# A ring of eight weight granules instead of four, with the low parts written over the raw weights

## What is computed

```python
u = rms_norm(h, mix_norm_pre[layer]); u = even_mixer(...) or odd_mixer(...)   # u @ w_in, attention, @ w_out
h = h + rms_norm(u, mix_norm_post[layer])
u = swiglu(rms_norm(h, ffn_norm_pre[layer]), w_gate, w_up, w_down)
h = h + rms_norm(u, ffn_norm_post[layer])
...
# third layer
hn = rmsnorm(h, norm_gain); proj = hn @ w_in
ya = pool_mixer(...) * silu(pool_gate); yb = ssm_mixer(...) * silu(ssm_gate)   # gelu, @ w_glu, sigmoid inside
h = h + concat([ya, yb]) @ w_out
h = h + (p @ w_ple) * sigmoid(h @ w_ple_gate)
return rmsnorm(h, final_gain)
```

## Time and profile before

| | |
|---|---|
| median of 3 executions | 3060.84 us (3059.07 to 3060.97) |
| span of the profiled execution | 3056.1 us, 3.0 to 4.9 us below the three times |
| PE busy | 2929.4 us, 96% of the span |
| DVE, ACT busy | 1733.2 us (57%), 1417.3 us (46%) |
| DMA | 515.45 MB, 169 GB/s over the span |
| granted TensorE clock | 0.986 on average |

### The profile page before, as it was taken

One profiled execution on the slowest core, in us unless ns is written; L12 is line 12 of the kernel. 1 busy time (PEld: TensorE's weight loads), 2 busy tenths in 40 slices (PEclk: granted clock), 3 DMA queues, 4 the chain that ended last, 5 costly groups with the idle time before them and its releaser, 6 DMA issues.

```text
span 3056.1 us, 34851 instructions
## 1 busy us (share of the span) xinstructions
PE 2929.4 (96%) x13709; PEld 2409.1 (79%) x13709; DVE 1733.2 (57%) x2222; ACT 1417.3 (46%) x1809; POOL 74.0 (2%) x66
## 2 busy tenths in 40 slices
PE   8999999999999999999999999999999998888998
PEld 7878878788888888878877788888888876656776
DVE  5775655544544454554445544544445569988545
ACT  5543375544444444454446544444444454343444
POOL 0000000000000000000000000000000021210000
PEclk9999999999999999999999999999999999989999
DMA  6532235555555555555552555555555553324543
GB/s 232 176 125 93 87 138 196 179 191 185 190 193 193 193 180 192 193 178 186 187 178 97 181 198 189 182 193 192 193 192 192 181 176 112 97 91 159 179 154 124
DMA packets 255293, 515.45 MB, mean 169 GB/s; under 512 B 8240, under 2 KB 8464, under 8 KB 254144
## 3 DMA queue, kind: packets, MB, share of 16 engines
q1 hardware_dynamic: 252896, 501.61, 48.4%
q0 software_dynamic: 2272, 12.10, 1.1%
HBM read 511.58 MB, written 2.10 MB: 168 GB/s over the span
## 4 chain that ended last, share of the span: by engine, by line
PE 86%; DVE 9%; ACT 3%; issue 2%; DMA 0%; SPq 0%; DVEq 0%; ACTq 0%
PE acc L464 79%; PE side L655 2%; DVE u L1606 2%; DVE u L2207 1%; DVE pc L1606 1%; DVE wlo L1618 1%; ACT ar L1006 1%; DVE ar L1606 1%; PE side L521 1%; DVE ar L1609 1%; PE side L766 1%; ACT whi L1017 1%; PE side L550 1%; ACT xh L1006 0%; ACT L1006 0%
## 5 line engine op out<-in xcount | busy, mean ns | idle before, releaser
L1618 DVE TENSOR_TENSOR wlo<-raw,whi 128x1024 fp32r<-128x1024 f32 x948 | 1156.4, 1226 | 1124.0 <-ACT whi L1017 1123.1
L1017 ACT ACTIVATE whi<-raw 128x1024 fp32r<-128x1024 f32 x948 | 997.9, 1060 | 1232.0 <-PE acc L464 1230.8
L464 PE MATMUL acc<-whi,xh 128*128 128x512 f32 x3072 | 1220.6, 397 | 55.6 <-DVE wlo L1618 49.3
L464 PE MATMUL acc<-whi,xl 128*128 128x512 f32 x3072 | 1204.4, 392 | 0.0
L464 PE MATMUL acc<-wlo,xh 128*128 128x512 f32 x3072 | 1204.1, 392 | 0.0
L464 PEld LDWEIGHTS acc<-whi,xh 128*128 128x128 f32 x3072 | 582.2, 190 | 187.6 <-DVE wlo L1618 37.3
L464 PEld LDWEIGHTS acc<-whi,xl 128*128 128x128 f32 x3072 | 581.5, 189 | 123.5
L464 PEld LDWEIGHTS acc<-wlo,xh 128*128 128x128 f32 x3072 | 582.5, 190 | 117.1
L464 PE MATMUL acc<-whi,hTh 128*128 128x512 f32 x720 | 281.1, 390 | 2.7 <-ACT u L1006 2.7
L464 PE MATMUL acc<-wlo,hTh 128*128 128x512 f32 x720 | 280.8, 390 | 0.0
L464 PE MATMUL acc<-whi,hTl 128*128 128x512 f32 x720 | 280.8, 390 | 0.0
(11 more groups left out here) (227 smaller groups left out, 1345.2 us busy)
## 6 DMA issues: line engine op xcount, KB each, us to landing
raw<-in_ffn_w_gate SPq DMA_DIRECT2D x88, 1024.0 KB, 5.0
raw<-in_ffn_w_up SPq DMA_DIRECT2D x88, 1024.0 KB, 5.0
raw<-in_ffn_w_down SPq DMA_DIRECT2D x88, 1024.0 KB, 5.0
raw<-in_ev_w_in SPq DMA_DIRECT2D x56, 1024.0 KB, 4.9
raw<-in_od_w_in SPq DMA_DIRECT2D x48, 1024.0 KB, 5.1
raw<-in_w_in SPq DMA_DIRECT2D x32, 1024.0 KB, 5.4
raw<-in_ev_w_out SPq DMA_DIRECT2D x16, 1024.0 KB, 5.0
raw<-in_od_w_out SPq DMA_DIRECT2D x16, 1024.0 KB, 5.0
```

What stands on the lines that cost most here:

```text
L464: mm = pe.matmul(acc[2 * pair + t][:], x[:, k0 + j, tok], w[:, ring, j], start=first and j == 0 and n == 0, stop=last and j == 1 and n == 2)
L1017: act.activation(whi[:, place % RING], raw_granule(place), ACT.Copy).then_inc(S("hi_done"), 1)
L1618: dve.tensor_tensor(wlo[:, place % RING], raw_granule(place), whi[:, place % RING].bitcast(F32), ALU.subtract).then_inc(S("lo_done"), 1)
```

## The change

The low parts get no tile of their own: DVE writes them over the raw weights they were made from. The room that becomes free goes to the high parts, so that `whi` holds eight granules. `raw` still has four slots of two granules each (SLOTS), and a slot is loaded again only when PE has used both its granules (`used`, where `lo_done` was). ACT may split granule g once PE has used g-8, if its slot has landed. The place of evacuations and leads, `after`, goes from 2 to 4 in ACT's and DVE's `granules`; ev_sb keeps its own value of 3 on ACT, and the up stages have their places written out (2) and keep them. In glu, with 4 granules in a chunk, the place becomes 3.

```diff
-RING = 4
+SLOTS = 4
+RING = 2 * SLOTS
...
-        raw = sb("raw", [RING, 4, CH])
+        with nc.sbuf_tensor("wlo", [P, RING, 2, CH], F32R) as wlo:
+            pass
+        raw = sb("raw", [RING, 2, CH])
         whi = sb("whi", [RING, 2, CH], F32R)
-        wlo = sb("wlo", [RING, 2, CH], F32R)
...
-                ring = n % RING if ring is None else ring
-                if not isinstance(n, int) or n >= RING:
-                    sp.wait_ge(S("lo_done"), 2 * n - 2 * RING + 2)
-                sp.dma_start(raw[:, ring], src).then_inc(S(f"landed{ring}"), 16)
+                ring = n % SLOTS if ring is None else ring
+                if not isinstance(n, int) or n >= SLOTS:
+                    sp.wait_ge(S("used"), 2 * n - RING + 2)
+                sp.dma_start(raw[:, 2 * ring:2 * ring + 2].rearrange("p g k n -> p (g k) n"), src)\
+                    .then_inc(S(f"landed{ring}"), 16)
...
-                                sp.wait_ge(S("lo_done"), 2 * (n0 + m) - 2 * RING + 2)
-                            sp.dma_start(raw[:, (n0 + m) % RING, 2 * c:2 * c + 2], w[:, 2 * m + c])\
+                                sp.wait_ge(S("used"), 2 * (n0 + m) - RING + 2)
+                            sp.dma_start(raw[:, 2 * ((n0 + m) % SLOTS) + c], w[:, 2 * m + c])\
...
                 if not isinstance(g, int) or g >= RING:
                     act.wait_ge(S("used"), g - (RING - 1))
-                act.activation(whi[:, place % RING], raw_granule(place), ACT.Copy).then_inc(S("hi_done"), 1)
+                act.activation(whi[:, place], raw_granule(place), ACT.Copy).then_inc(S("hi_done"), 1)
...
-            def granules(name, evac, lead, aside=None, after=2):
+            def granules(name, evac, lead, aside=None, after=4):
...
-                dve.tensor_tensor(wlo[:, place % RING], raw_granule(place), whi[:, place % RING].bitcast(F32),
+                dve.tensor_tensor(wlo[:, place], raw_granule(place), whi[:, place].bitcast(F32),
                                   ALU.subtract).then_inc(S("lo_done"), 1)
...
-            def granules(name, evac, lead, aside=None, after=2):
+            def granules(name, evac, lead, aside=None, after=4):
```

More of the change, by code:

```diff
@@ L244, in _ @@
                                                       bass.ds(first * CH + i * CH, CH)]
-                            slot(n0 + m + 8 * i, src, m % RING)
+                            slot(n0 + m + 8 * i, src, m % SLOTS)
                 elif name == "ple":
@@ L263, in raw_granule @@
         def raw_granule(place):
-            return raw[:, place // 2, 2 * (place % 2):2 * (place % 2) + 2]
+            return raw[:, place]
         def landed(eng, g):
@@ L272, in landed @@
             else:
-                before = sum(1 for k in range(GRAN0["ple"] // 2, GRAN0["pg"] // 2) if k < n and k % RING == n % RING)
-                eng.wait_ge(S(f"landed{n % RING}"), 16 * (n // RING + 1 - before))
+                before = sum(1 for k in range(GRAN0["ple"] // 2, GRAN0["pg"] // 2) if k < n and k % SLOTS == n % SLOTS)
+                eng.wait_ge(S(f"landed{n % SLOTS}"), 16 * (n // SLOTS + 1 - before))
         def tab(ct):
@@ L786, in block_of @@
                                 features_use(name, h)(0, j)
-                            granule(i * 16 + (g0 + 8 * m + j), j % RING, m, xh, xl, 2 * j, j == 0, j == 7)
+                            granule(i * 16 + (g0 + 8 * m + j), j, m, xh, xl, 2 * j, j == 0, j == 7)
                 block_of(0, True)
@@ L1011, in split @@
                 if place is None:
-                    place = g % (2 * RING)
+                    place = g % RING
                     if g % 2 == 0 or GRAN0["ple"] <= g < GRAN0["pg"]:
@@ L1331, in block_of @@
                                 n = (g0 + 8 * m + j) // 2
-                                act.wait_ge(S(f"landed{n % RING}"), i * 32 + 16 * (n // RING + 1))
+                                act.wait_ge(S(f"landed{n % SLOTS}"), i * 32 + 16 * (n // SLOTS + 1))
                             split(i * 16 + (g0 + 8 * m + j), j)
@@ L1614, in split @@
             def split(g, place=None):
-                place = g % (2 * RING) if place is None else place
+                place = g % RING if place is None else place
                 dve.wait_ge(S("hi_done"), g + 1)
-                dve.tensor_tensor(wlo[:, place % RING], raw_granule(place), whi[:, place % RING].bitcast(F32),
+                dve.tensor_tensor(wlo[:, place], raw_granule(place), whi[:, place].bitcast(F32),
                                   ALU.subtract).then_inc(S("lo_done"), 1)
```

## The result

The changed kernel takes 3065.11 us (median of 20 runs, 3059.85 to 3069.15), the kernel before, run between them, 3060.06 us (20 runs, 3057.68 to 3062.42). The ratio is 1.0016, with a 95% interval of 1.0010 to 1.0022: slower by 5.05 us. The interval tells that from none, though it is less than the 6.1 us that the forecast took for about what a measurement of this kernel can tell from none. The prediction was 3065.5 us.

A forecast was written before the change was run, and what follows sets the result against it. PE, busy 96% of the span, was taken as the bound, with only about 127 us idle to touch. Terms -7.5 + 7.5 - 2.8 + 1.1 + 4.9 + 1.5 = +4.7 us gave 3065.5 us, own range 3059 to 3071.

The forecast's parts named there:

- the steady state: Up and dn stages: PE does not wait there now, so the deeper ring brings 0.
- Delta rule: Beside ev_sb: ACT's splits no longer held up, copies start when their source is ready; -7.5 us, bounds 0 and -11.2.
- rival D: Delta rule: copies start early but PE then waits for DVE in the same places; sum +12.2, 3073 us, chance 0.15.
- Leads: Stage starts od_in, s_in, od_out, ev_out, s_out: leads come later, behind granule 4's split; together +7.5 us, bounds 0 and 10.
- splits behind them: Behind the leads: two more splits are ready, so waits such as 0.79 us at od_in's granule 3 go; -2.8 us.
- s_in's chunk 0: s_in, chunk 0: the evacuation comes behind a split and PE's turn waits for it; +1.1 us, which stays.
- it lands at T0 - 0.5: Leads: the slot of granules 4 and 5 lands 0.5 us before T0, the end of the stage before.
- Rival E: Up and dn stages: slot loads now and then take 9 us or more and stall PE; 3078 us, chance 0.12.
- glu's chunk 2: glu: glu_out(1) goes behind pool_group(3) and one split, so PE waits longer; +4.9 us, bounds 3.7 and 6.2.
- The clock: glu: after its longer idle spell PE begins chunk 2 at the lower clock level; +1.5 us, 0 to 3.4.
- rival B: Leads and half of glu's loss are hidden, delta rule gives its full 11.2 us; -10.4, 3050 us, chance 0.14.
- Rival C: s_in's state space rounds: eight PE waits of 4.7 us would go; -37, 3024 us, chance 0.04.

The follow-up runs named there:

- experiment 4: The changed kernel with evacuations and leads behind granule 2 and ACT splitting granule g only when g-4 is used: 3060.14 us, ratio 0.9999 to the kernel before.
- experiment 2: The changed kernel with evacuations and leads back behind granule 2 everywhere, ring of eight kept: 3050.15 us, ratio 0.9969 to the kernel before.
- experiment 5: The kernel before, with ACT's two copies of a turned ev_sb chunk put ahead of the split of granule 6: 3056.16 us, ratio 0.9987.
- Experiment 1: The changed kernel with the evacuations of glu alone back behind granule 2: 3056.89 us, ratio 0.9987 to the kernel before.
- experiment 8: The kernel before, ring of four, with only glu's evacuation and lead moved behind granule 4, a chunk's last: 3070.78 us, ratio 1.0036.
- experiment 7: The changed kernel with evacuations and leads behind granule 3 up to the second feed-forward, behind granule 2 from s_in on: 3047.26 us, ratio 0.9961.
- experiment 3: The changed kernel with evacuations and leads behind granule 3 everywhere: 3054.2 us, ratio 0.9980 to the kernel before.
- experiment 6: The changed kernel with GpSimd's loads of x and c_odd, which ran beside ev_out's first weights, issued later: 3060.96 us, ratio 1.0003 to the kernel before.

## Why the prediction was right, point by point

**The subtraction in place, 0, and the steady state, 0: right.** 1221 ns a split, and experiment 4, which keeps both, is at 0.9999 of before.

**Delta rule, -7.5: right in its mechanism, too small, and bounded by a row read wrongly.** The stages show -10.2 us, experiment 2 -10.7 by medians, and experiment 4 that ACT's held splits were the cause. The bound of 11.2 us took the earlier trace rows for PE's idle time, where they add that of the weight loads to that of the matmuls: for the matmuls ACT's two parts were 7.7 us, in five places. The "three places" for DVE were one pause counted twice, at 207.7 us, and the weight loads' side of a pause that the matmuls' side puts down to ACT's copy, at 310.1. PE's idle time in this part fell by 8.8 us (12.9 to 4.2), more than the 7.7, and its busy time by 1.4, which no row here explains. The step that was mis-sized is "where its chain ends just behind ACT's copy, little is won", for which I had taken a third off. There is one such place, at 310.1 us, and experiment 5, where PE still waits 1.28 us there, shows that it counts while the ring is one of four. With the ring of eight it does not, and at 207.7 us DVE's wait falls from 2.11 to 0.92. That DVE's own splits come earlier, since ACT's do, and that so its chain starts earlier is argued, not shown step by step; experiments 4 and 5 show that it hangs on ACT's held splits and not on the five pairs of copies. So rival D, whose premise was that DVE would hold PE in the same places, is refuted for the new ring; it had got a chance of 0.15.

**Leads, +7.5, splits behind them, -2.8, and s_in's chunk 0, +1.1: the sum of +5.8 was near, the parts were not all.** By PE's waits, od_in has +2.0 us (forecast 1.9), s_in +2.0 (2.2) and s_out +1.7 (1.7). od_out has nothing (0.6): PE waits 0.31 us there in both kernels. ev_out has +3.1 (1.1). The waits for a split behind the leads, 0.79 us twice and 0.43 three times, are gone: -2.9. In s_in, ACT makes PE wait 1.04 us before the turn, as forecast, yet "it stays" was wrong: a wait of 1.1 us at granule 17 went in exchange. That is +5.8 in all, the forecast's sum, with ev_out's excess of 2.0 us made up by od_out and s_in. The step that failed is "it lands at T0 - 0.5": I used the median of 48 loads in another stage for a slot that meets 2.4 MB of GpSimd's, and it landed at 475.4 us, 1.2 us behind ev_z's last matmul. Rival E had such late loads, of 9 us, but spread over the up and dn stages; it came where a lead hung on it. Its price of 3078 follows from neither of its two sums, +47 and +5.

**glu's chunk 2, +4.9: right.** 4.51 us, ending on the DVE instruction named.

**The clock, +1.5: too small.** Experiments 1 and 8 put 2.4 to 2.7 us on glu's spell alone. Ahead of it I had no term at all: ev_out's spells brought 1.9 us behind them, in a stretch at a granted 0.81, and s_out's were followed by +0.8, with 0.79 granted from 2844 to 2852 us. Experiment 1 makes the move in glu worth 8.2 us by medians and 6.9 in the stages, where the two terms together had 6.4.

In medians the change is made of the ring, -10.7 (experiment 2), the places outside glu with their clock, +6.7 (experiment 1 less 2), and glu with its clock, +8.2 (the changed kernel less experiment 1). These add up to +4.3, as before ran at 3060.84 us beside them. Beside the forecast's -7.5, +5.8 and +6.4, each is larger than I had it, the gain by 3.2 us and the losses by 2.7 together. Nothing in the forecast made these two equal: that the total came out right to half a microsecond is luck. Of rival B, the delta rule's part came nearly whole and the hidden leads not at all. Rival C's rounds kept waits of 3.8 to 5.4 us.

What stays open is small: why experiment 7 beats experiment 2 by 2.9 us where I had expected 1.0 from the stages (of which, at s_in's first matmul, only 0.4 is left between experiments 3 and 2), and the differences of some tenths to a microsecond in the feed-forward stages and in od_in, where no wait of PE differs. I take these for stretches at the lower clock, which come in one execution and not in the next; that was not tried.

## What to carry to other kernels

When one edit bundles two changes, price them apart: here the deeper ring was worth -10.7 us and the later evacuation +15.0, and the kernel that keeps the first and mends the second beats both. A split that waits for a buffer holds back every short copy behind it on its engine: the order of two copies and a split alone was worth 3.8 us. Before a list of waits becomes a bound, ask which queues it counts: matmuls and weight loads together show one pause twice. And ask of each lead which slot's landing now stands ahead of it: the median time of landing is no bound for a load that runs beside another queue's.

## What the runs showed of the hardware that was not expected

A load of 1 MB issued by SyncE, whose medians are 5.0 to 5.4 us to landing, took 9.4 us beside a load of 2 MB and one of 384 KB issued by GpSimd (9.6 and 8.9 us in experiments 2 and 3), and 5.1 us with these two elsewhere (experiment 6).

The granted clock fell behind idle spells of quite different shape. One spell of 2.79 us in glu left it at 1.00. One of 7.30 us was followed by a granted 0.57 over 6 us. And two short ones, 2.01 and 1.68 us, at ev_out were followed by a granted 0.81 in a stretch of 10 us in which PE was busy throughout. Such a loss is in no list of waits, and only the granted clock shows it. TensorE: Matmul & The Clock Gate of the Trainium skill, "Part 1: The HAM clock gate", has the two levels, 1.2 and 2.4 GHz, and says that how many matmuls run at the lower one varies between runs of one kernel. The runs here agree in so far as the changed kernel's 20 times scatter over 9.3 us, those of before over 4.7, and the mean granted clock is 0.983 in the changed kernel's shortest run and 0.980 in its longest.
